# Two float32 transformer layers on one core: input sums on VectorE, T3 ahead of z, and the modulation pairs at other places

## The chip, the cores and the metric

The kernel runs on one core of a Trainium2 chip. The metric is the device time of one execution in microseconds. Before the change it is 1578.08 us, the median of three runs (1577.12 to 1578.24).

## What is computed

512 tokens of width 1024, float32, go through two layers.

```
x -> rmsnorm -> x @ w_in -> gated spatial unit, 8 heads of attention (q, k, v, gates g_a, g_b)
  -> merged @ w_out -> x + rmsnorm(.)
  -> rmsnorm -> (silu(h @ w_gate) * (h @ w_up)) @ w_down -> x + rmsnorm(.)          # first feed-forward, 2816 hidden
mod = silu(c) @ mod_w + mod_b       # 6144 values: shift1, scale1, gate1, shift2, scale2, gate2
  -> rmsnorm * (1 + scale1) + shift1 -> h @ w_in_2 -> short convolution, stick-breaking attention, SSD scan
  -> sum of three branches, each times a sigmoid gate -> @ w_o -> x + gate1 * rmsnorm(.)
  -> rmsnorm * (1 + scale2) + shift2 -> (silu(gt) * up) @ w_ffn_out -> x + gate2 * rmsnorm(.)   # second feed-forward
```

The first layer is `first_block`, the second `hybrid_layer` with its modulation vector `mod`, which depends only on `c` and so can be computed at any time before its parts are used.

## The kernel before

**Weights as a stream of units.** All large weights pass through two buffers of 8 KB per partition. A unit is loaded by SyncE into `raw`; ScalarE rounds it into `w_hi` (L1100), VectorE subtracts to get the rest, `w_lo` (L1585, semaphore `lo_done`), and TensorE multiplies in three passes, hi by hi, hi by lo and lo by hi (L2295 to L2297). A unit of 256 columns is two feature tiles of 24 matmuls each. TensorE executes its instructions in program order, and so does each other engine; semaphores tie them together. No planner is at work: the order of each engine is written out by hand.

**Feed-forward up stages.** Of the 22 units of `up` (and of `up2` in the second layer) the first four are multiplied plainly: two in `first_pair`, where token halves are interleaved with the normalisation, then two in `f_pairs`. `tile` in VectorE's `hidden` multiplies gate and up parts of one of these. The other 18 (m = 0 to 17) take seven products of 2x2 blocks instead of eight (`blocks` on TensorE, L2382 on; each product is 12 matmuls of 256 columns at L2389 to L2391). This needs sums of the input's quarters, S1 to S4 in `s_sum`, made once per stage, and sums T1 to T4 of each unit's weight blocks: T1 and T3 on VectorE (`t1_part` L1729, `t3_part` L1735), T2 and T4 on GpSimd (L993, L997). `sums_lo` (L1751) waits for both. `p1` to `p7` are the products, in the order of `pe_order`; z, c21, c22 and m are VectorE's additions of products (L1813, L1818, L1824, L1829 and L1797). Before p3 of unit m TensorE waits for c22 of m, and c22 stands behind `sums_lo` of m + 1 in VectorE's order. `dve_order` and `act_order` count these steps for the waits of other engines.

**Input sums.** Before, VectorE makes S1 (three operations, L1770 to L1772) ahead of everything else of the stage, and GpSimd makes S3, S2 and S4 (seven operations of 128x1024, L977 to L985).

**Modulation.** `mod` is computed on GpSimd in six pairs of 512 columns. `mod_begin` clears the sum and loads the bias and the first slab; each of 16 `mod_step`s loads the next slab (a GpSimd DMA, L939), waits for its own, multiplies (L957) and adds (L960). The last step of a pair raises `mod_summed`. TensorE then turns the sum (`mod_columns`, eight transposes, L2566, into banks 6 and 7) and VectorE reduces it to a column (`mod_columns`, L1700). One buffer, `mod_acc`, holds the running pair; it lies over memory that the SSD scan of the second layer uses until its last head is done. Pairs 0 and 2 give the two shift columns, pairs 1 and 3 the two scale columns; pairs 4 and 5 the gates, spread over the partitions by `mod_gate`.

**Where the pairs run before the change.** Pair 0 before the attention; pair 1 after it (eight steps, the roots of the layer norm at L1031 and L1032, five steps, then three in `blocks`); pair 2 inside the 18 units of the first up stage; pair 3 in the first down stage; pair 4 while the merge stage of the second layer runs; pair 5 inside the 18 units of the second up stage.

**Attention gates.** GpSimd adds 1 to the eight second gates (L1021) as they come, then multiplies the eight heads' outputs by them (L1024, `gated_b`). Only then does it begin pair 1.

**Merge stage.** Sixteen units: three gate units and one of the branch outputs (`branches`), four times. TensorE runs three gate units, then the first `branches`.

**Down stage and normalisation.** `post_norm` gives ScalarE's, VectorE's and GpSimd's steps around the residual additions. GpSimd's part is the roots (L894, L895). `hidden_hi` and `hidden_lo` (L1710) split hidden tiles 4 and 5 in the middle of the 18 units (at m == 8) and the others in the down stage.

## Time and profile before

| | us |
|---|---|
| median of three runs | 1578.08 |
| the profiled execution, its own time | 1577.7 |
| its span, first to last instruction | 1576.0 |
| TensorE busy | 1533.7 (97%) |
| VectorE busy | 1018.0 (65%) |
| GpSimd busy | 687.7 (44%) |
| ScalarE busy | 669.8 (43%) |
| granted TensorE clock, mean | 0.993 |

A matmul's record is longer than its distance to the next, so the busy time is no measure of speed; the waits of TensorE and the distances of its starts are. The 1.7 us between span and time lie around the program.

### The profile page before, as it was taken

How to read it: one execution, taken by the hardware profiler on the slowest of the kernel's cores; microseconds unless marked ns; L12 is line 12 of the kernel's file. 1: busy time of each engine (PE TensorE's matmuls, PEld its weight loads, DVE VectorE, ACT ScalarE, POOL GpSimd, SP SyncE). 2: the span in 40 equal slices, each digit the busy share in tenths (PEclk: the TensorE clock that was granted, in tenths of full speed). 3: DMA queues.
4: the chain of work that ended last, by engine and by line, in shares of the span. 5: the costliest groups of instructions: out<-in, count | busy, mean ns of one | idle time of the engine just before them, and what ended most of it. 6: DMA issues, size and time to landing. Idle time of an engine off the chain costs nothing.

```text
span 1576.0 us, 23248 instructions
## 1 busy us (share of the span) xinstructions
PE 1533.7 (97%) x8908; PEld 1346.1 (85%) x8908; DVE 1018.0 (65%) x1379; ACT 669.8 (43%) x1109; POOL 687.7 (44%) x543
## 2 busy tenths in 40 slices
PE   9999999979989999999999999999999899999998
PEld 9878788868889999988898888888889799999886
DVE  4342766447588999964276979643457799997423
ACT  6223444313454444442176775323236344544221
POOL 3871002760776656669120802691003666662000
PEclk9999999989999999999999999999999999999999
DMA  7532132422523434454322212443322243444231
GB/s 216 174 120 80 54 81 55 147 87 80 182 73 101 132 104 133 128 181 146 115 67 81 81 54 69 139 141 106 106 80 81 60 131 113 126 134 134 95 107 54
DMA packets 189620, 171.40 MB, mean 109 GB/s; under 512 B 20688, under 2 KB 162000, under 8 KB 189520
## 3 DMA queue, kind: packets, MB, share of 16 engines
q1 hardware_dynamic: 181456, 144.84, 30.6%
q0 software_dynamic: 8064, 25.20, 5.2%
q8 instruction: 67, 1.10, 0.3%
q14 instruction: 33, 0.27, 0.1%
HBM read 167.91 MB, written 2.10 MB: 108 GB/s over the span
## 4 chain that ended last, share of the span: by engine, by line
PE 70%; DVE 15%; POOL 9%; issue 4%; ACT 1%; DMA 0%; DVEq 0%; POOLq 0%; ACTq 0%
PE bank L2295 17%; PE bank L2297 17%; PE bank L2296 17%; POOL w_sum L997 3%; DVE w_lo L1751 3%; DVE act_m L1829 3%; POOL w_sum L993 2%; DVE w_lo L1742 2%; PE bank L2458 2%; PE bank L2459 2%; PE bank L2462 2%; DVE w_lo L1758 2%; DVE act_m L1729 1%; PE bank L2389 1%; PE bank L2616 1%
## 5 line engine op out<-in xcount | busy, mean ns | idle before, releaser
L1585 DVE TENSOR_TENSOR w_lo<-raw,w_hi 128x2048 fp32r<-128x2048 f32 (+1 forms) x109 | 216.3, 1985 | 239.4 <-ACT w_hi L1100 239.3
L2295 PE MATMUL bank<-h_hi,w_hi 128*128 128x512 f32 (+1 forms) x800 | 310.9, 389 | 11.1 <-DVE w_lo L1585 11.1
L2297 PE MATMUL bank<-h_hi,w_lo 128*128 128x512 f32 (+1 forms) x800 | 299.8, 375 | 0.0
L2296 PE MATMUL bank<-h_lo,w_hi 128*128 128x512 f32 (+1 forms) x800 | 299.6, 375 | 0.0
L1100 ACT CAST w_hi<-raw 128x2048 fp32r<-128x2048 f32 (+1 forms) x108 | 171.4, 1587 | 199.4 <-PE bank L2297 191.8
L957 POOL TENSOR_SCALAR mod_raw<-mod_raw,c_silu 128x512 f32<-128x512 f32 x96 | 197.0, 2053 | 19.3 <-DMA mod_raw<-in_mod_w 15.6
L2295 PEld LDWEIGHTS bank<-h_hi,w_hi 128*128 128x128 f32 x800 | 151.9, 190 | 40.0 <-DVE w_lo L1585 12.4
L2389 PE MATMUL bank<-s_hi,w_hi 128*128 128x256 f32 x576 | 166.7, 289 | 13.4 <-DVE act_m L1824 13.4
L2296 PEld LDWEIGHTS bank<-h_lo,w_hi 128*128 128x128 f32 x800 | 152.0, 190 | 27.4 <-issue 1.9
L2297 PEld LDWEIGHTS bank<-h_hi,w_lo 128*128 128x128 f32 x800 | 151.6, 189 | 27.7
L2391 PE MATMUL bank<-s_hi,w_lo 128*128 128x256 f32 x576 | 162.9, 283 | 0.0
L2390 PE MATMUL bank<-s_lo,w_hi 128*128 128x256 f32 x576 | 162.9, 283 | 0.0
L960 POOL TENSOR_TENSOR mod_acc<-mod_acc,mod_raw 128x512 f32<-128x512 f32 x96 | 138.1, 1438 | 8.3
L2389 PEld LDWEIGHTS bank<-s_hi,w_hi 128*128 128x128 f32 x576 | 110.2, 191 | 20.0 <-DVE act_m L1824 19.9
L2389 PE MATMUL bank<-h_hi,w_hi 128*128 128x256 f32 x432 | 122.4, 283 | 0.0
L2390 PE MATMUL bank<-h_lo,w_hi 128*128 128x256 f32 x432 | 122.2, 283 | 0.0
L2391 PE MATMUL bank<-h_hi,w_lo 128*128 128x256 f32 x432 | 122.1, 283 | 0.0
L2390 PEld LDWEIGHTS bank<-s_lo,w_hi 128*128 128x128 f32 x576 | 110.3, 192 | 0.0
L2391 PEld LDWEIGHTS bank<-s_hi,w_lo 128*128 128x128 f32 x576 | 110.3, 192 | 0.0
L2295 PE MATMUL bank<-w_hi,act_hi 128*128 128x512 f32 x280 | 109.0, 389 | 0.0
L2297 PE MATMUL bank<-w_hi,act_lo 128*128 128x512 f32 x280 | 108.9, 389 | 0.0
L2296 PE MATMUL bank<-w_lo,act_hi 128*128 128x512 f32 x280 | 108.9, 389 | 0.0
(476 smaller groups left out, 3348.3 us busy)
## 6 DMA issues: line engine op xcount, KB each, us to landing
raw<-in_w_in SPq DMA_DIRECT2D x102, 512.0 KB, 4.5
mod_raw<-in_mod_w POOLq DMA_DIRECT2D x96, 256.0 KB, 3.0
raw<-in_w_ffn_in SPq DMA_DIRECT2D x44, 512.0 KB, 4.9
raw<-in_w_gate SPq DMA_DIRECT2D x22, 512.0 KB, 4.0
raw<-in_w_up SPq DMA_DIRECT2D x22, 512.0 KB, 5.3
raw<-in_w_down SPq DMA_DIRECT2D x20, 512.0 KB, 4.5
raw<-in_w_ffn_out SPq DMA_DIRECT2D x20, 512.0 KB, 4.5
raw<-in_w_out SPq DMA_DIRECT2D x8, 512.0 KB, 4.3
```

Of the source, the lines that this page charges most:

```text
L957: then(gp.tensor_scalar(mod_raw[:, s, :], mod_raw[:, s, :], c_silu[:, k:k + 1], None, ALU.mult))
L960: ins = gp.tensor_tensor(acc, acc, mod_raw[:, s, :], ALU.add)
L997: gp.tensor_tensor(t4, t2, quarter_of(n, 1, 0), ALU.subtract).then_inc(block_pool, 1)
L1100: ins = act.copy(w_hi[s][:, cols], raw[s][:, cols])
L1585: ins = dve.tensor_tensor(w_lo[s][:, cols], raw[s][:, cols], w_hi[s][:, cols].bitcast(F32), ALU.subtract)
L1751: dve.tensor_tensor(operand_pair(w_lo, n0, 2), operand_pair(w_sum, n0, 2), operand_pair(w_hi, n0, 2).bitcast(F32), ALU.subtract).then_inc( ...
L2295: pe.matmul(o, st_hi, mv_hi, start=first, stop=False)
L2296: pe.matmul(o, st_hi, mv_lo, start=False, stop=False)
L2297: return pe.matmul(o, st_lo, mv_hi, start=False, stop=last)
L2389: pe.matmul(o, hi[:, k, :], mv_hi(k), start=first and k == 0, stop=False, skip_group_check=not first)
L2390: pe.matmul(o, hi[:, k, :], mv_lo(k), start=False, stop=False, skip_group_check=not first)
L2391: ins = pe.matmul(o, lo[:, k, :], mv_hi(k), start=False, stop=k == 3, skip_group_check=not first)
```

## The change

The input sums S1, S2 and S4 are made by VectorE, S1 behind the lo part of the stage's third unit, S2 and S4 behind that of the fourth; GpSimd keeps S3, and the last of its three operations waits for the third unit's lo part. In the loop of the 18 units VectorE makes T3 ahead of z. Hidden tiles 4 and 5 are split at the start of the down stage. GpSimd applies each gate as soon as its head is there. The modulation pairs move: nine steps of pair 1 ahead of the layer norm's roots, four behind, three in units m = 1 to 3 of the first loop; pair 2 in the first down stage; pair 3 between the SSD scan and pair 4, with two steps ahead of the scan's root and fourteen behind it; pair 5 begins behind the second layer's gate with four steps ahead of `post_norm(2)`, and its other twelve stand in m = 1 to 12 of the second loop. TensorE's and VectorE's `mod_columns` move accordingly: pair 1 at the end of the first loop, pair 2 in the first down stage, pair 3 directly ahead of the first `branches`.

```diff
-            yield from ("s1", "s1_lo", "s3_lo", "s24_lo", "t1 0", "t3 0", "pair 0", "sums 0", "t4 0", "t1_lo 0")
+            yield from ("s1", "s3_lo", "t1 0", "s24", "t3 0", "s1_lo", "pair 0", "s24_lo", "sums 0", "t4 0", "t1_lo 0")
...
-                yield from [f"t1 {ahead}"] if ahead else []
+                yield from [f"t1 {ahead}", f"t3 {ahead}"] if ahead else []
                 yield f"z {m}"
-                yield from [f"t3 {ahead}"] if ahead else []
...
-            def blocks(n0, which, c):
+            def blocks(n0, which, c, pair, done):
...
+                gp.wait_ge(lo_done, n0 + 3)
                 gp.tensor_tensor(s3, s3, h_quarter(h_lo, 1, 0), ALU.subtract).then_inc(block_pool, 1)
-                wait_dve(gp, which, "s1")
-                gp.tensor_tensor(s2, s1, h_quarter(h_hi, 0, 0), ALU.subtract).then_inc(block_pool, 1)
-                wait_pool_sum(gp, which, 2)
-                then(gp.tensor_tensor(s2, s2, h_quarter(h_lo, 0, 0), ALU.subtract))
-                then(gp.tensor_tensor(s4, h_quarter(h_hi, 0, 1), s2, ALU.subtract))
-                gp.tensor_tensor(s4, s4, h_quarter(h_lo, 0, 1), ALU.add).then_inc(block_pool, 1)
...
+                    if 1 <= m <= 2 * KD - done:
+                        mod_step(pair, done + m - 1)
...
                 then(gp.tensor_scalar(gates[:, KD + f, :], gates[:, KD + f, :], 1.0, None, ALU.add))
-            for f in range(KD):
                 gp.wait_ge(head_out, f + 1)
                 gp.tensor_tensor(q_t[:, f, :], q_t[:, f, :], gates[:, KD + f, :], ALU.mult).then_inc(gated_b, 1)
             mod_begin(1)
-            for i in range(8):
+            for i in range(9):
                 mod_step(1, i)
...
-            blocks(n_up, 0, 1)
-            mod_pair(3)
+            blocks(n_up, 0, 1, 1, 13)
+            mod_pair(2)
             post_norm(1)
...
+            mod_begin(3)
+            for i in range(2):
+                mod_step(3, i)
             gp.wait_ge(ms2_ready, 1)
...
+            for i in range(2, 2 * KD):
+                mod_step(3, i)
             mod_pair(4)
             mod_lo_part(4)
+            mod_begin(5)
+            for i in range(4):
+                mod_step(5, i)
             post_norm(2)
-            blocks(n_up2, 1, 3)
+            blocks(n_up2, 1, 3, 5, 4)
...
-                    if units == 6 and 1 <= j <= 4:
-                        for t in range(4 * j + 2, 4 * j + 6):
+                    if units == 6 and j <= 4:
+                        for t in range(4 if j == 0 else 4 * j + 2, 4 * j + 6):
...
-                    if m == 2 and which == 0:
-                        dve.wait_ge(small_in, 16 * (SMALL + SMALL_2))
-                        mod_columns(1, gain_3, True)
-                    if m == 8:
-                        hidden_lo(which, PLAIN)
-                        hidden_lo(which, PLAIN + 1)
...
             split(n_mg + 4)
+            mod_columns(3, gain_4, True)
             merge(n_mg, 0, 0, STILL)
...
             pe.wait_ge(ssm_lo_done, 4)
-            pe.wait_ge(mod_out, 4)
-            branches(n_mg + 3, STILL)
+            mod_columns(3)
+            branches(n_mg + 3, STILL, 4)
```

## Rows read from the trace of the kernel before

**Rows 1.** Page, part 1: busy time, share of the span and instructions of each engine.
```profile
PE 1533.7 (97%) x8908; PEld 1346.1 (85%) x8908; DVE 1018.0 (65%) x1379; ACT 669.8 (43%) x1109; POOL 687.7 (44%) x543
```

**Rows 2.** Waits of TensorE: line and releaser, us in total, times, longest.
```profile
PE bank L2389 <- DVE act_m L1824: 13.4, 32, 1.3
PE bank L2295 <- DVE w_lo L1585: 11.1, 2, 6.6
PE bank L2660 <- DVE v_sgu L1945: 9.0, 1, 9.0
```

**Rows 3.** Timeline of GpSimd, 820 to 1200 us: start, duration, instruction, idle before.
```profile
979.37 3.21 POOL L1069 TENSOR_TENSOR z_t<-z_t 128x512 f32<-128x512 f32 x1
...
990.92 1.68 POOL L1071 TENSOR_TENSOR rr_ssm<-ms_ssm,power 128x8 f32<-128x8 f32 x1 [8.34 <-DVE ms_ssm L2238]
992.55 0.96 POOL L944 MEMSET mod_acc<- 128x1024 f32 x1
...
1000.31 1.57 POOL L957 TENSOR_SCALAR mod_raw<-mod_raw,c_silu 128x512 f32<-128x512 f32 x1 [4.30 <-DMA mod_raw<-in_mod_w]
...
1004.19 2.65 POOL L957 TENSOR_SCALAR mod_raw<-mod_raw,c_silu 128x512 f32<-128x512 f32 x1
...
1069.12 1.70 POOL L960 TENSOR_TENSOR mod_acc<-mod_acc,mod_raw 128x512 f32<-128x512 f32 x1
```

**Rows 4.** Timeline of TensorE, 985 to 1020 us: first matmul of the first branch unit.
```profile
1012.94 0.39 PE L2295 MATMUL bank<-sb_hi,w_hi 128*128 128x512 f32 x1
```

**Rows 5.** Windows: stretch, length, busy of PE, PEld, DVE, ACT, POOL, PEclk, DMA, GB/s.
```profile
461.00:470.00 9.00, 8.49 (x30) 6.85 (x31) 8.34 (x5) 1.25 (x2) 8.84 (x3) 0.81 0.44 118
```

**Rows 6.** Timeline of GpSimd, 215 to 360 us: gate products and pair 1.
```profile
284.35 14.14 POOL L1024 TENSOR_TENSOR q_t<-q_t,gate_a 128x512 f32<-128x512 f32 x8
...
337.79 1.26 POOL L960 TENSOR_TENSOR mod_acc<-mod_acc,mod_raw 128x512 f32<-128x512 f32 x1
```

**Rows 7.** Timeline of VectorE, 280 to 362 us: the last head's output.
```profile
286.14 0.69 DVE L1898 COPY q_t<-bank 128x512 f32<-128x512 f32 x1 [3.30 <-PE bank L2639]
```

**Rows 8.** Timeline of TensorE: first matmul of the third unit, both up stages.
```profile
461.51 0.67 PE L2295 MATMUL bank<-h_hi,w_hi 128*128 128x512 f32 x1 [4.42 <-DVE w_lo L1585]
...
1232.15 0.80 PE L2295 MATMUL bank<-h_hi,w_hi 128*128 128x512 f32 x1 [6.63 <-DVE w_lo L1585]
```

**Rows 9.** Timeline of VectorE, 440 to 540 us: an operation of S1.
```profile
448.08 3.31 DVE L1771 TENSOR_TENSOR s_sum<-s_sum,h_lo 128x1024 f32<-128x1024 f32 x1
```

**Rows 10.** Timeline of VectorE and GpSimd inside the first loop.
```profile
498.25 0.42 DVE L1829 TENSOR_TENSOR act_m<-act_m,silu_t 128x256 f32<-128x256 f32 x1
...
536.03 1.72 DVE L1735 TENSOR_TENSOR w_sum<-raw 128x512 f32<-128x512 f32 x1
...
539.01 1.23 DVE L1751 TENSOR_TENSOR w_lo<-w_sum,w_hi 128x1024 fp32r<-128x1024 f32 x1 [0.93 <-POOL w_sum L997]
...
541.75 1.34 POOL L960 TENSOR_TENSOR mod_acc<-mod_acc,mod_raw 128x512 f32<-128x512 f32 x1
541.86 1.51 DVE L1829 TENSOR_TENSOR act_m<-act_m,silu_t 128x256 f32<-128x256 f32 x1
```

**Rows 11.** Timeline of TensorE, 535 to 560 us: the end of p2 and the start of p3.
```profile
539.95 0.28 PE L2390 MATMUL bank<-h_lo,w_hi 128*128 128x256 f32 x1
540.07 0.28 PE L2391 MATMUL bank<-h_hi,w_lo 128*128 128x256 f32 x1
540.62 0.39 PE L2389 MATMUL bank<-s_hi,w_hi 128*128 128x256 f32 x1 [0.28 <-DVE act_m L1824]
```

**Rows 12.** Chain of waits in order of time: T2 of two neighbouring units around m = 8.
```profile
578.32 1.31 POOL w_sum L993
...
590.12 1.30 POOL w_sum L993
```

**Rows 13.** Timelines around the second layer's output projection: gate product, first root.
```profile
1165.94 0.39 PE L2574 MATMUL bank<-mod_lo,ones_r 128*128 128x512 f32 x1
...
1186.19 0.32 POOL L894 TENSOR_SCALAR sq_y<-sq_y 128x1 f32<-128x1 f32 x1 [23.77 <-ACT y_out L1106]
```

More of the change, by code:

```diff
@@ L672, in act_order @@
         def act_order():
-            yield from ("s1_hi", "s3_hi", "s24_hi", "pair 0", "sums 0", "p1 0", "t4 0", "t1 0")
+            yield from ("s3_hi", "s1_hi", "pair 0", "s24_hi", "sums 0", "p1 0", "t4 0", "t1 0")
             for m in range(BLOCKS):
@@ L694, in wait_pool @@
         def wait_pool(eng, which, m, total):
-            eng.wait_ge(block_pool, (2 * BLOCKS + 3) * which + 2 * m + 3 + total)
-        def wait_pool_sum(eng, which, done):
-            eng.wait_ge(block_pool, (2 * BLOCKS + 3) * which + done)
+            eng.wait_ge(block_pool, (2 * BLOCKS + 1) * which + 2 * m + 1 + total)
         POST_UNIT = [n_out + 3, n_dn + 11, n_out2 + 3, n_dn2 + 11]
@@ L1033, in _ @@
             gp.wait_ge(merged, KD)
-            for i in range(8, 13):
+            for i in range(9, 13):
                 mod_step(1, i)
             post_norm(0)
-            blocks(n_up, 0, 1)
-            mod_pair(3)
+            blocks(n_up, 0, 1, 1, 13)
+            mod_pair(2)
             post_norm(1)
@@ L1251, in hidden @@
                 split(n0 + 2)
-                wait_dve(act, which, "s1")
-                act.copy(s_hi[:, S1], s_sum[:, S1]).then_inc(block_act, 1)
-                wait_pool_sum(act, which, 1)
+                wait_pool(act, which, 0, 0)
                 act.copy(s_hi[:, S3], s_sum[:, S3]).then_inc(block_act, 1)
@@ L1257, in hidden @@
                 split(n0 + 3)
-                wait_pool_sum(act, which, 3)
-                act.copy(s_hi[:, S2:S4 + 1], s_sum[:, S2:S4 + 1]).then_inc(block_act, 1)
+                wait_dve(act, which, "s1")
+                act.copy(s_hi[:, S1], s_sum[:, S1]).then_inc(block_act, 1)
                 tile(n0 + 2, act_hi[:, 2, :], 0, STILL)
                 pair_hi(0)
+                wait_dve(act, which, "s24")
+                act.copy(s_hi[:, S2:S4 + 1], s_sum[:, S2:S4 + 1]).then_inc(block_act, 1)
                 sums_hi(0)
@@ L1638, in post_norm @@
                 for j in range(units):
-                    if units == 6 and 1 <= j <= 4:
-                        for t in range(4 * j + 2, 4 * j + 6):
+                    if units == 6 and j <= 4:
+                        for t in range(4 if j == 0 else 4 * j + 2, 4 * j + 6):
                             hidden_lo(k // 2, t)
@@ L1772, in hidden @@
                 dve.tensor_tensor(s1, s1, h_quarter(h_lo, 1, 1), ALU.add).then_inc(block_dve, 1)
-                tile(n0, 0, 0)
-                split(n0 + 2)
-                wait_act(dve, which, "s1_hi")
-                wait_pool_sum(dve, which, 2)
-                dve.tensor_tensor(s_lo[:, S1], s1, s_hi[:, S1].bitcast(F32), ALU.subtract).then_inc(block_dve, 1)
+                tile(n0 + 1, 1, 1)
                 wait_act(dve, which, "s3_hi")
                 dve.tensor_tensor(s_lo[:, S3], s_sum[:, S3], s_hi[:, S3].bitcast(F32), ALU.subtract).then_inc(block_dve, 1)
-                tile(n0 + 1, 1, 1)
                 split(n0 + 3)
+                t1_part(0)
+                wait_dve(dve, which, "s1")
+                then(dve.tensor_tensor(s2, s1, h_quarter(h_hi, 0, 0), ALU.subtract))
+                then(dve.tensor_tensor(s2, s2, h_quarter(h_lo, 0, 0), ALU.subtract))
+                then(dve.tensor_tensor(s4, h_quarter(h_hi, 0, 1), s2, ALU.subtract))
+                dve.tensor_tensor(s4, s4, h_quarter(h_lo, 0, 1), ALU.add).then_inc(block_dve, 1)
+                tile(n0 + 2, 2, 0)
+                t3_part(0)
+                wait_act(dve, which, "s1_hi")
+                dve.tensor_tensor(s_lo[:, S1], s1, s_hi[:, S1].bitcast(F32), ALU.subtract).then_inc(block_dve, 1)
+                pair_lo(0)
                 wait_act(dve, which, "s24_hi")
@@ L2437, in blocks @@
                     product(m, 6, "x", *sums(S4), first=False)
-                    if m == 0 and which == 0:
-                        mod_columns(1)
             def token_unit(n, x_hi, x_lo, k0, first, last, pace, width=512, tiles=range(NT)):
@@ L2561, in mod_columns @@
                 pe.wait_ge(mod_summed, pair + 1)
-                if pair == 2:
-                    pe.wait_ge(mod_out, 2)
                 for q in range(KD):
@@ L2848, in gate_unit, with branches @@
                     feature_tile(n, f, pace)
-            def branches(n, pace):
+            def branches(n, pace, columns=0):
                 u = UNITS[n]
@@ L2857, in branches @@
                     wait(pe, emptied[2 + f], u["round"] + pace.by(pace.rounds))
+                    if f == 1:
+                        wait(pe, mod_out, columns)
                     for b, k0, x_hi, x_lo, kt in ((4 + 2 * f, 2, sb_hi, sb_lo, 2), (5 + 2 * f, 4, ssm_hi, ssm_lo, 4), (2 + f, 0, sc_hi, sc_lo, 2)):
```

41 lines of the change are left out of this document (11 added, 30 removed).

## The prediction

> **What bounds the kernel now.** I read the page first, then who waited for whom, then the timelines at each wait, and last the chain. TensorE is busy for 97% of the span [rows 1], so what can be won is the time it stands, and what can be lost is a new stand. Its waits are few [rows 2]: 32 short ones before p3 (13.4 us, 0.42 us each), one at the third unit of either up stage (11.1 us), and one before the spatial products (9.0 us). The timelines say what makes each, and the code says which new waits stand in TensorE's own order. There is one, and it decides.
>
> **1. Pair 3 ahead of the first branch unit (the largest term, a loss).** TensorE now turns pair 3 directly ahead of the first `branches`, and that wait wants all 16 steps of it. GpSimd can't begin before its last square sum of the SSD scan, which ends at 979.37 + 3.21 = 982.6 us [rows 3]: `mod_acc` lies over the scan's states, and it is one in-order queue. TensorE reaches the first branch unit at 1012.9 us [rows 4], only 30 us later. What GpSimd has to do in between:
> - Begin: from clearing the sum to the first product 1000.31 - 992.55 = 7.8 us, of which 4.3 are the wait for the slab [rows 3]. Bounds 3.5 and 7.8; I take 7.8, the same act ten microseconds later.
> - The root for the scan, now in the midst of it: 1.7 us [rows 3].
> - Sixteen steps. Pair 4 took from 1000.31 to 1069.12 + 1.70, 70.5 us, 4.4 a step; the first was 3.9 from the next [rows 3]. The longer ones have VectorE's lo parts beside them. For most of this stretch TensorE and so VectorE will stand, so I take 3.9 and add three collisions of about 1 us, without the last step's load: 64.8 us. Bounds 62 and 70.5.
> Together 982.6 + 7.8 + 64.8 + 1.7 = 1056.9 us in the old frame, bounds 1049.8 and 1062.6. TensorE waits 1056.9 - 1012.9 = 44.0 us (37 to 50). The eight transposes are only moved. Behind TensorE's wait are queued the whole merge stage and all that follows; nothing covers it. The root's delay of some 6 us, which VectorE and TensorE wait for, ends inside this stand and costs nothing more.
> After a stand the granted clock is at its lower level of 1.2 GHz for a while: 0.81 in mean over the 9 us behind the wait of 4.4 us [rows 5], so 9 x 0.19 = 1.7 us are lost. I add 1.7. Sum of the part: **+45.7 us**.
>
> **2. The gates head by head.** Before, the eight products start behind the last gate and end at 284.35 + 14.14 = 298.5 us, 1.8 each [rows 6]. Seven of them can now be done earlier; the last waits for the last head, 286.14 + 0.69 = 286.8 us [rows 7], and ends at 288.6. Pair 1 begins 9.9 us earlier, but one more step (4.1) is in front of the roots, so GpSimd turns to them 5.8 us earlier than 337.79 + 1.26 = 339.1 us [rows 6]. TensorE's wait of 9.0 us [rows 2] falls to 3.2. Then TensorE is late by that still, as GpSimd's roots are last again. **-5.8 us**, bounds 3.5 (more collisions, as the steps meet other VectorE work) and 10.7 (the wait and the slow clock behind it gone).
>
> **3. The input sums.** VectorE's S1 operations, 3.31 us beside GpSimd's [rows 9], leave the way of the third unit. Its lo part can then be ready when TensorE is done with the pair, where the two waits began, at 461.51 - 4.42 = 457.1 and 1232.15 - 6.63 = 1225.5 us [rows 8]. That would save their 11.1 us [rows 2] and the slow clock behind each, 1.7 as above [rows 5]: 14.5 us. But the work is not gone. Between that point and the first p3, VectorE now has seven operations of 1024 columns at 1.2 us (the lo part of the sums, [rows 10]) = 8.6, where it had three, and its two-input operations collide: one with S3's last operation, which now waits for the same lo part (2.1 us, 3.31 - 1.2), two with T2 and T4 (1 us each, as T3's 1.72 in [rows 10] against 0.7 for its size). With the tiles, lo parts and first operands that were always there I get an estimated 30 us of VectorE work until p7 of the first unit. TensorE has 96 matmuls of 512 columns at 0.23 us (twice the 0.12 of 256 columns, [rows 11]) and 24 of 256 to do until then, 25 us. VectorE is late by about 5 us, shared out over p1, p7, p6, p5 and p3, of which about 0.3 a stage were there before: 14.5 - 10.0 + 0.6 is **-5.1 us** (bounds 0 and 14.5). The new wait on GpSimd queues S3's last operation and T2 of unit 0 behind it; ScalarE waits for S3 ahead of the second tile, which is in the 5 us.
>
> **4. The loops.** One unit is 84 matmuls, 0.12 us apart [rows 11] = 10.08 us. TensorE loses 540.62 - 540.07 - 0.12 = 0.43 us before p3 and another 0.1 on the restart, 0.53 in all, so a unit takes 10.61. The reason is a ring: T4 on GpSimd, the lo part of the sums (it stood 0.93 us for T4), c22, and back over a step of a pair: VectorE's L1829 takes 1.51 us because GpSimd's add holds it up, and 0.42 where no step runs [rows 10]. Without a step T1, T2 and T4 come 1.1 us earlier, more than the 0.53 that are missing, and TensorE is the bound. Steps stood in 16 units of either loop; now in 3 and in 12. In the first loop 13 stands go, in the second 4: 17 x 0.53 = 9.0 us. The next ring, over the weights' load and the first operands' lo part, I take to be shorter than 10.08 us; rival two says what it costs if it isn't.
> The two hidden tiles at m == 8 made that unit 590.12 - 578.32 = 11.80 us long [rows 12], 1.2 above its neighbours, in both loops: -2.4. The column of pair 1 at m == 2 is two operations of the same 512 columns, so 1.2 again: -1.2. All of these return in the down stage, where TensorE's plain units keep it busy for 10.9 us each and VectorE has only their lo part to make; they cost nothing there, and without that cover the same 3.6. Since small waits for loads will take back a part I count 12.2 of the 12.6. Sum **-12.2 us**, bounds 5 and 13.
>
> **5. T3 ahead of z.** T3 took 1.72 us since it met T2 on GpSimd [rows 10]. Put first it takes about 0.7, but T2 then starts behind it. T4 ends when T1, T3, T2 and T4 are through one after the other, whichever goes first: 0, bounds -0.2 and +0.2 a unit in the 15 units with a step, 3 us in all. z moves back by 0.6 us and TensorE's p5 waits for it; no wait of TensorE at z is in the trace [rows 2]. By the Trainium skill (SBUF — State Buffer, on the shared port pair) a VectorE operation with two SBUF inputs and a GpSimd operation exclude each other for a whole instruction. That gives the 0 above; were it a sharing of bandwidth, T3 alone first would give each unit up to 1 us, 3 + 12 units at most 0.53 = 8 us. The durations here, 0.42 or 1.51 for one operation, speak for the lock.
>
> **6. Pair 5's four steps ahead of post_norm(2).** They can begin when the gate product is read, 1165.94 + 0.39 = 1166.3 us, and take 7.8 + 4 x 4 = 23.8 us, to 1190.1; the first root was asked for at 1186.19 [rows 13]. Four microseconds late, of which part is slack: **+0.5 us**, bounds 0 and 3.
>
> **The sum.** 45.7 + 0.5 - 5.8 - 5.1 - 12.2 = +23.1 us on the profiled execution's 1577.7 us: 1600.8. It stood 0.4 below the median of the runs, 1578.08, so 1601.2; I say **1601 us**.
>
> **Rivals.**
> - **TensorE does not stand for pair 3, the other side.** If GpSimd had pair 3 summed when TensorE arrives, the gains alone would be left: 1577.7 - 23.1 + 0.5 = 1555.1 us. The place is the wait ahead of the first branch unit, the price 45.7 us. It decides from the point at which 16 steps fit in 30 us, that is 1.4 us a step with a begin of 7.8; the shortest distance of two steps is 3.9 [rows 3]. For it speaks only that I could have misread what the wait counts. Chance 0.04.
> - **The stand comes, the gains don't.** VectorE, with the sums back, keeps the start of both loops late by all that it saved, and the loops stay at 10.6 us by another ring (the raw load's), so that only the gates' 5.8 and the 3.6 are won: 1577.7 + 46.2 - 9.4 = 1614.5 us. Chance 0.12. For it: VectorE stood only 0.93 us a unit [rows 10], so it has little to spare. Against it: where L1829 took 0.42 us TensorE did not stand in that unit, and only 32 of 36 units have the wait [rows 2].
> - **The stand is shorter and the gains full.** 38.7 us by the low bounds, gains 30: 1586 us. Chance 0.06.
>
> **How the numbers follow.** The forecast case has 0.78. Its own bounds (37 to 50 us of stand, gains of 17 to 30) reach from about 1588 to 1612; both extremes at once are unlikely. The range 1589 to 1615 takes in the second rival and leaves out the first, most of the third and the tails. Below 0.2% (3.2 us, about what a measurement of this kernel can tell from no change) lie only the first rival and a part of what I have not thought of: faster 0.05, same 0.01, slower 0.94.
>
> **What would show it.** In the changed kernel's profile: a wait of TensorE of 37 to 50 us at the transposes L2566's line, released by GpSimd's L960, and a granted clock of 0.5 behind it; the wait before the spatial products at 3 us; none at the third units, but some at the first products of the loops; units of 10.08 us from m = 4 on in the first loop and from 13 on in the second, 10.6 before. The forecast is wrong if TensorE's largest wait isn't the one at pair 3, or if it is far from 44 us.

## The result, and the profile after

The changed kernel takes **1604.74 us** (median of four runs, 1604.25 to 1605.91) beside 1577.63 us for the kernel before on the same chip. The ratio is 1.0173, with an interval of 1.0155 to 1.019: 27.1 us slower, where 1601 us had been forecast. The profiled execution spans 1602.5 us, at a mean granted TensorE clock of 0.984.

Page of the changed kernel, part 1 (busy time, share of the span and instructions of each engine), which answers to [rows 1]:

```profile
PE 1531.8 (96%) x8908; PEld 1344.2 (84%) x8908; DVE 963.6 (60%) x1387; ACT 672.4 (42%) x1109; POOL 654.4 (41%) x535
```

VectorE and GpSimd are less busy than before, by 54 and 33 us. Eight operations have moved from GpSimd to VectorE, which is quicker at them (in the first stage the four took 2.4 to 4.3 us on GpSimd before and take 1.2 to 2.2 on VectorE now), and fewer of the two engines' operations meet. The time is longer all the same. Who waited for whom, TensorE alone, in the changed kernel (line and releaser, us in total, times, longest), to be read beside [rows 2]:

```profile
PE bank L2542 <- POOL mod_acc L954: 37.6, 1, 37.6
PE bank L2369 <- DVE act_m L1808: 6.9, 16, 0.8
PE bank L2636 <- DVE v_sgu L1923: 6.6, 1, 6.6
PE bank L2855 <- DVE rr_diag L2221: 3.1, 1, 3.1
PE bank L2369 <- DVE w_lo L1723: 2.4, 2, 1.2
PE bank L2369 <- ACT act_m L1258: 2.2, 2, 1.1
PE bank L2559 <- POOL ident L882: 1.6, 1, 1.6
PE bank L2369 <- ACT silu_t L1231: 1.3, 2, 0.7
...
PE bank L2369 <- DVE w_lo L1732: 0.5, 2, 0.2
```

The first line is the new stand: TensorE's transposes of pair 3 wait for GpSimd's last add. Of the old waits the two at the third units (11.1 us) are gone, the 32 before p3 have become 16, and the one before the spatial products fell from 9.0 to 6.6. New are 3.1 us before the products that spread the SSD root, and the four last kinds at L2369, all at the first products of either loop.

TensorE runs the same 8908 instructions in both kernels and only `mod_columns` moves. So the account can be made from the start of one and the same matmul in either trace, and the difference. Timeline of TensorE in the changed kernel (start, duration, instruction, idle before):

```profile
343.94 3.76 PE L2636 MATMUL bank<-w_sp_t,v_sgu 128*128 128x128 f32 x16 [6.59 <-DVE v_sgu L1923]
...
487.62 0.39 PE L2369 MATMUL bank<-h_hi,w_hi 128*128 128x256 f32 x1 [1.08 <-ACT act_m L1258]
...
991.29 2.56 PE L2855 MATMUL bank<-rr_diag,ones 128*128 128x128 f32 x16 [3.10 <-DVE rr_diag L2221]
...
1043.46 1.94 PE L2542 MATMUL bank<-ident,mod_acc 128*128 128x128 f32 x8 [37.62 <-POOL mod_acc L954]
1045.05 0.78 PE L2275 MATMUL bank<-sb_hi,w_hi 128*128 128x512 f32 x1
```

| matmul | before | after | after less before | term of the sum | forecast | found |
|---|---|---|---|---|---|---|
| output of attention, nothing changed yet | 261.9 | 262.9 | +1.0 | (scatter) | 0 | +1.0 |
| spatial products | 345.0 | 343.9 | -1.1 | gates | -5.8 | -2.1 |
| third unit, ten matmuls in | 465.3 | 457.9 | -7.4 | | | |
| first loop, behind its starting waits | 490.8 | 487.6 | -3.2 | sums, stage one | | -2.1 |
| last p3 of the first loop | 669.5 | 657.4 | -12.2 | first loop | | -9.0 |
| first branch unit, six matmuls in | 1014.1 | 1047.3 | +33.2 | pair 3 | +45.7 | +45.4 |
| third unit of the second stage, ten in | 1235.7 | 1260.7 | +24.9 | | | |
| second loop, behind its starting waits | 1261.8 | 1290.6 | +28.8 | sums, stage two | (both) -5.1 | -4.4 |
| last p3 of the second loop | 1428.9 | 1455.5 | +26.6 | second loop | (both) -12.2 | -2.2 |

Between pair 3 and the second stage's third unit the difference stays at +33.2: pair 5's four steps cost nothing (0.5 forecast). The found terms add up to 26.6 us; the two spans differ by 26.5. Eight transposes (0.8 us at full clock) have left the first loop, and eight now stand ahead of the first branch unit. So 0.8 of the loop's 9.0 us and 0.8 of pair 3's 45.4 are work that moved, neither won nor lost.

### The profile page after: what moved, and what is told of

It reads as the page before. It is cut to its first block and busy times, and to the rows that moved or that the text cites. A ratio compares the mean times of both kernels' runs of the same rounds, so it can differ in the third digit from the quotient of the medians.

```text
span 1602.5 us, 23250 instructions
## 1 busy us (share of the span) xinstructions
PE 1531.8 (96%) x8908; PEld 1344.2 (84%) x8908; DVE 963.6 (60%) x1387; ACT 672.4 (42%) x1109; POOL 654.4 (41%) x535
## 5 line engine op out<-in xcount | busy, mean ns | idle before, releaser
L1566 DVE TENSOR_TENSOR w_lo<-raw,w_hi 128x2048 fp32r<-128x2048 f32 (+1 forms) x109 | 212.7, 1952 | 232.4 <-ACT w_hi L1084 232.3
L951 POOL TENSOR_SCALAR mod_raw<-mod_raw,c_silu 128x512 f32<-128x512 f32 x96 | 193.2, 2012 | 21.7 <-DMA mod_raw<-in_mod_w 17.9
L2369 PE MATMUL bank<-s_hi,w_hi 128*128 128x256 f32 x576 | 165.4, 287 | 8.7 <-DVE act_m L1808 6.9
L980 POOL TENSOR_TENSOR w_sum<-raw,act_m 128x512 f32<-128x512 f32 x36 | 55.1, 1529 | 227.7 <-PE bank L2371 150.2
L2369 PE MATMUL bank<-h_hi,w_hi 128*128 128x256 f32 x432 | 122.6, 284 | 4.5 <-DVE w_lo L1723 2.4
L2369 PEld LDWEIGHTS bank<-s_hi,w_hi 128*128 128x128 f32 x576 | 110.3, 192 | 12.8 <-DVE act_m L1808 10.1
```

Of the source, the lines that this page charges most:

```text
L951: then(gp.tensor_scalar(mod_raw[:, s, :], mod_raw[:, s, :], c_silu[:, k:k + 1], None, ALU.mult))
L980: gp.tensor_tensor(t2, quarter_of(n, 1, 1), four(t1_sum(m)), ALU.subtract).then_inc(block_pool, 1)
L1566: ins = dve.tensor_tensor(w_lo[s][:, cols], raw[s][:, cols], w_hi[s][:, cols].bitcast(F32), ALU.subtract)
L2369: pe.matmul(o, hi[:, k, :], mv_hi(k), start=first and k == 0, stop=False, skip_group_check=not first)
```

## The experiments

Each kernel was timed beside the kernel before on its own chip, where that took 1579 to 1580 us instead of 1577.6; so ratios are given, and for parts of a few microseconds the starts of the same matmuls in two traces, as above.

**1. The root's delay inside the stand** (run root_first), from the changed kernel:

```diff
             mod_begin(3)
-            for i in range(2):
-                mod_step(3, i)
             gp.wait_ge(ms2_ready, 1)
             gp.tensor_tensor(rr_ssm[:], ...).then_inc(rr_ready, 1)
...
-            for i in range(2, 2 * KD):
+            for i in range(2 * KD):
                 mod_step(3, i)
```

> The changed kernel with the root of the SSD norm ahead of all sixteen steps of pair 3 instead of behind two of them; GpSimd does the same work in another order. In the changed kernel's trace TensorE waits 3.1 us for that root and runs about 1.6 us slower behind the wait, and then stands 37.6 us for pair 3. Theory A, as in the prediction (the root's delay ends inside the stand): the end of the stand is set by GpSimd's queue alone, so TensorE arrives 4.7 us earlier and stands 4 to 5 us longer (41 to 43 us); the time stays at 1604.7 us within 1. Rival B (the two waits are paid one after the other): 4.7 us less, 1600.0 us.

Measured: 1604.74 us (1603.67 to 1606.76), ratio 1.0165 [1.0147, 1.0183]. TensorE's waits in it:

```profile
PE bank L2540 <- POOL mod_acc L954: 43.7, 1, 43.7
```

The wait for the root is gone and the stand has grown from 37.6 to 43.7 us, by 6.1. Of these, 5.0 are what the root cost (3.1 us of wait and 1.9 by which the matmuls behind it fell back further, a short lag and then the lower clock), 0.8 come from a TensorE that was already ahead when it reached the root, and 0.3 from a pair that ended later. Behind the stand the starts of the same matmuls agree to 0.1 us in the two traces. So a wait ahead of a stand is free, as the prediction said, and theory B falls. It also says that the stand can't be shortened from TensorE's side: its end is GpSimd's.

**2. The transposes 33 us later** (run cols_later). The first turn of the merge's loop is written out on TensorE and VectorE, and pair 3's column stands in it:

```diff
-            mod_columns(3)
-            branches(n_mg + 3, STILL, 4)
-            with pe.Fori(0, 3) as p:
+            branches(n_mg + 3, STILL)
+            for g in range(3):
+                gate_unit(n_mg + 4 + g, STILL)
+            mod_columns(3)
+            branches(n_mg + 7, STILL, 4)
+            with pe.Fori(0, 2) as p:
```

> The changed kernel with TensorE's transposes of pair 3 and VectorE's column of it moved behind the next three gate units of the merge (33 us later); GpSimd's order stays. Theory A (the stand is the whole of the loss, and the gains stand by themselves): 40.7 us go (37.6 of wait and 3.1 of slow clock behind it), 1604.7 - 40.7 = 1564.0 us, range 1562 to 1568. Pair 4 then ends about 1127 us, ahead of its gate product near 1158. Rival B (the stand had covered GpSimd's and VectorE's work, which now meets in the merge stage; a wait comes back at the new place or at pair 4's gate product): 1575 us or more, with a wait of 10 us or more there.

Measured: 1565.78 us (1563.66 to 1566.63), ratio 0.9911 [0.9894, 0.9929]; from the changed kernel's 1.0173 that is 41 us, and by the starts of the same matmuls 39.4. TensorE's longest waits:

```profile
PE bank L2373 <- DVE act_m L1808: 7.5, 16, 1.1
PE bank L2640 <- DVE v_sgu L1923: 6.6, 1, 6.6
PE bank L2859 <- DVE rr_diag L2221: 3.1, 1, 3.1
```

The transposes in its timeline:

```profile
1050.21 1.09 PE L2546 MATMUL bank<-ident,mod_acc 128*128 128x128 f32 x8
```

The transposes come at 1050.21, GpSimd's last add ended at 1050.16, and TensorE's unit before them at 1050.15. So there is no stand, but only just: here the pair ends 7 us later than in the changed kernel, and 33 us of delay were barely enough. There is none at pair 4's gate product either. One wait was the whole loss, and the gains stand by themselves: the changed kernel with this one edit is faster than the kernel before.

**3. Both edits** (run cols_later_root_first), the two diffs together.

> Both edits: pair 3's transposes behind three gate units, and the root ahead of all steps. Theory A: without the stand the root's 3.1 us of wait and 1.6 us of slow clock are on TensorE's path and now go: 4.7 us less than with the transposes alone, 1559.3 us. Sixteen steps end near 1043 us and TensorE comes at about 1047, so no new wait. Rival B (what the root costs is paid by the later steps, pair 3 ends behind TensorE's arrival): no less than with the transposes alone, 1564 us or more, with a wait at the transposes.

Measured: 1566.83 us (1565.83 to 1568.65), ratio 0.9923 [0.9905, 0.994]. Theory B:

```profile
PE bank L2544 <- POOL mod_acc L954: 5.8, 1, 5.8
```

The root's 3.1 us are gone and 5.8 us at the transposes have come. I had counted pair 3's steps as in the stand, with VectorE mostly silent. Here VectorE works on in the merge stage, the steps collide with it, and the pair ends at 1048.5 us instead of 1043. Run root_first has the same operations in the same order: from clearing the sum to the last add they took 74.1 us there, where VectorE was silent from 1010 to 1040 us, and 79.9 us here. The length of a GpSimd chain depends on what VectorE does beside it.

**4. All pairs where they were, the other edits kept** (run pairs_back):

```diff
-                    if 1 <= m <= 2 * KD - done:
-                        mod_step(pair, done + m - 1)
+                    if which == 0:
+                        if m == 0:
+                            mod_step(1, 14)
+                            mod_step(1, 15)
+                        elif m == 1:
+                            mod_begin(2)
+                        else:
+                            mod_step(2, m - 2)
+                    elif m == 0:
+                        mod_begin(5)
+                    elif m <= 2 * KD:
+                        mod_step(5, m - 1)
```

> The changed kernel with every modulation pair where it was before (pair 1's last steps, pair 2 and pair 5 in the loops, pair 3 in the down stage, eight steps ahead of the attention's roots, pair 1's column at the third unit), but with the other edits kept: gates head by head, input sums, T3 ahead of z, the two hidden tiles out of the ninth unit. Theory A (the parts add up): gates about 6.6 less since only eight steps stand ahead of the roots, sums 6.5, hidden tiles 2.4, T3 0: 1577.6 - 15.5 = 1562 us, range 1559 to 1566, with units of 10.6 us wherever a step runs. Rival B (T3 ahead of z is what shortens the units, not the steps' absence): units of 10.1 to 10.3 us with steps in them and 1550 to 1556 us. Rival C (the gains at the start of the loops need GpSimd free of steps there): 1567 us or more.

Measured: 1565.3 us (1563.43 to 1568.44), ratio 0.9913 [0.9891, 0.9934], 14.3 us less than the kernel before; 15.5 had been expected. TensorE's waits:

```profile
PE bank L2374 <- DVE act_m L1812: 12.7, 32, 0.8
PE bank L2374 <- DVE w_lo L1727: 3.8, 2, 2.6
PE bank L2645 <- DVE v_sgu L1930: 2.7, 1, 2.7
```

The p3 of three neighbouring units of the first loop, in TensorE's timeline:

```profile
555.77 0.39 PE L2374 MATMUL bank<-s_hi,w_hi 128*128 128x256 f32 x1 [0.33 <-DVE act_m L1812]
566.44 0.39 PE L2374 MATMUL bank<-s_hi,w_hi 128*128 128x256 f32 x1 [0.34 <-DVE act_m L1812]
577.11 0.39 PE L2374 MATMUL bank<-s_hi,w_hi 128*128 128x256 f32 x1 [0.34 <-DVE act_m L1812]
```

With the steps back the 32 waits are back, and a unit takes 10.67 us although T3 stands ahead of z. That refutes theory B and shows what shortened the units: the missing steps. Against the kernel before, the first loop gains 0.2 us here, 9.0 in the changed kernel. The start of stage one, counted from where the clock is full again behind the spatial products, keeps only 0.1 us of the sums' gain, against 1.9 with the steps gone (one first product waits 2.64 us for its lo part): a part of theory C.

**5. Seven steps ahead of the attention's roots** (run seven_steps), on top of run cols_later:

```diff
-            for i in range(9):
+            for i in range(7):
                 mod_step(1, i)
...
-            for i in range(9, 13):
+            for i in range(7, 11):
                 mod_step(1, i)
...
-            blocks(n_up, 0, 1, 1, 13)
+            blocks(n_up, 0, 1, 1, 11)
```

> On top of the kernel with pair 3's transposes moved later (run cols_later): seven steps of pair 1 ahead of the attention's roots instead of nine, four behind the merge of the first output, five instead of three in the first loop. It tests what term 2 of the prediction missed: the gates' edit gave 2.4 us of wait where 5.8 were forecast, because the ninth step took 5.9 us and not 4.1. Theory A (GpSimd's roots alone set that wait): TensorE's wait of 6.6 us before the spatial products goes to below 0.5, the slow clock behind it too, about 7.0 less there; two more steps in the loop cost at most 2 x 0.53 = 1.1 us. 5.9 us less than cols_later in all, 1560 us beside a kernel before at 1579.6. Rival B (VectorE's or ScalarE's chain is right behind the roots): the wait stays above 2.5 us, and the gain is below 3.5 us.

Measured: 1557.7 us (1557.38 to 1558.72), ratio 0.9869 [0.9852, 0.9885]. By the traces the spatial products start 6.5 us earlier, 1.9 more come back with the clock behind them, and the loop's two steps cost 0.9: 7.5 us at the end of the first loop. Further on the trace gains another 1.6 us that this edit doesn't explain. It has the same wait of 3.1 us for the SSD root, but the granted clock does not fall behind it (the mean there is 1.00; the same stretch of the changed kernel, 985 to 995 us, has 0.88). Windows as in [rows 5]:

```profile
978.00:988.00 10.00, 6.91 (x39) 5.72 (x38) 7.40 (x12) 3.00 (x3) 9.45 (x7) 1.00 0.48 148
```

That makes 9.1 us by the traces, 6.6 by the ratios. Theory A: GpSimd's roots alone set the wait, and nothing else is close behind them.

**6. One step ahead of the SSD root, the transposes in the midst of the branch unit** (run one_step_split), on top of run cols_later:

```diff
-            for i in range(2):
-                mod_step(3, i)
+            mod_step(3, 0)
...
                     if f == 1 and columns:
+                        mod_columns(3)
                         wait(pe, mod_out, columns)
```

> On top of cols_later: one step of pair 3 ahead of the SSD root instead of two, and TensorE's transposes between the two halves of the next branch unit instead of ahead of it (5.5 us later). With no step ahead of the root and the transposes where they were, the wait for the root went and one of 5.8 us at the transposes came. Theory A: the root is given at about 982 us instead of 986.4, so the 3.1 us of wait and 1.6 us of slow clock go; pair 3 ends near 1050 as before, TensorE comes to the transposes at 1051; in their place it waits some 2 us for VectorE's sum of the columns, which banks 6 and 7 need. 2.5 to 3 us less than cols_later. Rival B (the wait for VectorE's columns or pair 3's end takes it all back): no difference.

Measured: 1560.95 us (1560.36 to 1561.87), ratio 0.989 [0.9873, 0.9906]. Timeline of TensorE:

```profile
1047.56 1.03 PE L2545 MATMUL bank<-ident,mod_acc 128*128 128x128 f32 x8
1050.18 0.50 PE L2278 MATMUL bank<-sb_hi,w_hi 128*128 128x512 f32 x1 [1.58 <-DVE gain L1684]
```

The wait for the root is gone, that for VectorE's column is 1.58 us. Behind the attention stage the traces differ by 3.0 us (a shorter wait before the spatial products comes on top, in which the two kernels are the same); the ratios differ by 0.0021, 3.3 us: theory A.

**7. T3 behind z again** (run t3_back on top of run cols_later, and run best_t3_back on top of run best, below):

```diff
                         t1_part(m + 1)
-                        t3_part(m + 1)
...
                     dve.tensor_tensor(g[:, 256:512], region(m, "x"), mid[:, 256:512], ALU.add).then_inc(block_dve, 1)
+                    if m + 1 < BLOCKS:
+                        t3_part(m + 1)
```

> cols_later with T3 of the next unit behind z again, as in the kernel before; all else kept. Theory A (as in the prediction, T3's place is worth nothing): the same time within 1 us, units without a step stay at 10.08 us. Rival B (the units' 0.53 us came from T3 being ahead, not from the missing steps): units of 10.6 us again, 9 us or more slower than cols_later.

Measured: 1561.84 us (1560.92 to 1563.26), ratio 0.9895 [0.9878, 0.9911]. The units without a step keep their 10.08 us, so T3's place is not what shortened them; but this is less than cols_later, not more (2.5 us by the ratios), and by its trace 1.4 of it lie in the loops (0.5 in the first, 1.0 in the second). The more exact pair of runs:

> The kernel of run best with T3 behind z again. The earlier run t3_back came out 3.9 us below cols_later, but its trace gives T3 behind z at most 1.0 us, all in the second loop, and the rest lies in the attention stage, where the kernels are the same. Theory A (T3's place is worth 1 us at most): 0 to 1.2 us less than best. Rival B (T3 ahead of z costs what the earlier medians differ by): 3 to 4 us less.

Measured: 1553.34 us (1552.6 to 1553.46), ratio 0.9835 [0.9822, 0.9849], beside 1555.28 for run best: 1.9 us. By the traces 0.4 us come in the first loop and 1.0 in the second. One unit of the second loop in run best, VectorE and GpSimd:

```profile
1275.69 0.68 DVE L1715 TENSOR_TENSOR w_sum<-raw 128x512 f32<-128x512 f32 x1
...
1279.08 1.22 DVE L1731 TENSOR_TENSOR w_lo<-w_sum,w_hi 128x1024 fp32r<-128x1024 f32 x1 [1.91 <-POOL w_sum L984]
...
1275.90 1.63 POOL L980 TENSOR_TENSOR w_sum<-raw,act_m 128x512 f32<-128x512 f32 x1 [3.42 <-DVE act_m L1709]
1277.67 1.30 POOL L984 TENSOR_TENSOR w_sum<-w_sum,raw 128x512 f32<-128x512 f32 x1
```

And the same unit in run best_t3_back:

```profile
1273.34 1.72 DVE L1716 TENSOR_TENSOR w_sum<-raw 128x512 f32<-128x512 f32 x1
...
1276.31 1.22 DVE L1732 TENSOR_TENSOR w_lo<-w_sum,w_hi 128x1024 fp32r<-128x1024 f32 x1 [0.92 <-POOL w_sum L985]
...
1273.22 1.29 POOL L981 TENSOR_TENSOR w_sum<-raw,act_m 128x512 f32<-128x512 f32 x1 [3.42 <-DVE act_m L1710]
1274.65 1.56 POOL L985 TENSOR_TENSOR w_sum<-w_sum,raw 128x512 f32<-128x512 f32 x1
```

T3 ahead saves VectorE a microsecond (0.68 us instead of 1.72), but T2 then takes 1.63 us instead of 1.29. T2 and T4 together need 3.07 us against 2.99, and VectorE only waits longer for T4, 1.91 us instead of 0.92. A unit with a step takes 10.67 us with T3 ahead and 10.60 with T3 behind.

**8. The input sums as before** (run sums_back), on top of run cols_later: S2 and S4 on GpSimd, S1 ahead of the third unit's lo part.

```diff
-                gp.wait_ge(lo_done, n0 + 3)
                 gp.tensor_tensor(s3, s3, h_quarter(h_lo, 1, 0), ALU.subtract).then_inc(block_pool, 1)
+                wait_dve(gp, which, "s1")
+                gp.tensor_tensor(s2, s1, h_quarter(h_hi, 0, 0), ALU.subtract).then_inc(block_pool, 1)
+                wait_pool_sum(gp, which, 2)
+                then(gp.tensor_tensor(s2, s2, h_quarter(h_lo, 0, 0), ALU.subtract))
+                then(gp.tensor_tensor(s4, h_quarter(h_hi, 0, 1), s2, ALU.subtract))
+                gp.tensor_tensor(s4, s4, h_quarter(h_lo, 0, 1), ALU.add).then_inc(block_pool, 1)
```

> cols_later with the input sums as in the kernel before (S2 and S4 on GpSimd, S1 ahead of the third unit's lo part on VectorE); all else kept. From the two traces the input sums' edit was worth 2.1 us in the first and 4.4 us in the second up stage. Theory A: 6.5 us more than cols_later, with waits of 4.4 and 6.6 us at the third units and none worth naming before the first p1. Rival B (with no steps in the loop's head, the old order would have cost less in the first stage): 4 to 5 us more. Rival C (VectorE pays back all of it): no difference.

Measured: 1569.33 us (1568.25 to 1571.68), ratio 0.9942 [0.9924, 0.996]; the ratios differ by 0.0031, 4.9 us. TensorE's waits:

```profile
PE bank L2286 <- DVE w_lo L1577: 11.0, 2, 6.6
```

The third units wait again, and the starting waits of the loops are gone, as theory A had it. By the starts of the same matmuls the edit is worth 1.9 us up to the first loop and 4.5 up to the second. But with the sums on VectorE the first units of the loops are longer, by 0.3 and 0.7 us, so that 1.6 and 3.8 are left, 5.4 in all. The size lies between A (6.5) and B (4 to 5), and the ratios' 4.9 us is B's.

**9. The sum of it** (run best): the edits of runs cols_later, one_step_split and seven_steps together.

> All that the runs so far speak for: the changed kernel with pair 3's transposes between the halves of the second branch unit, one step ahead of the SSD root, and seven, four and five steps of pair 1. Theory A (the parts add up, each sits at its own wait): seven_steps' 1557.7 us less the 3.4 us that the traces give one_step_split behind the attention: 1554.3 us beside a kernel before at 1578.9, a ratio of 0.984 to 0.986. Rival B (a later wait takes part of it back, since GpSimd has pair 4's 16 steps and the gate product still ahead): 1556 us or more.

Measured: **1555.28 us** (1555.2 to 1556.04), ratio 0.9848 [0.9835, 0.9861]. The parts add up to a microsecond. What is missing is no later wait, as rival B has it: in the trace of run seven_steps the slow clock behind the root was already absent, so that one_step_split's edit could win only 1.2 us there by the traces, not 3.0. With T3 behind z the kernel takes 1553.34 us, 26 us less than the kernel before.

**10. The gates behind the last head again** (run best_gates_back):

```diff
                 then(gp.tensor_scalar(gates[:, KD + f, :], gates[:, KD + f, :], 1.0, None, ALU.add))
+            for f in range(KD):
                 gp.wait_ge(head_out, f + 1)
```

> The kernel of run best with the eight gate products behind the last gate again. Theory A (GpSimd's queue sets the roots, and the products come 6.5 us later there: they end at 298.4 us in the kernel before and at 291.9 with the edit): with seven steps pair 1's part ends near 335.2 us where the first root is wanted at 332.0, so a wait of some 3.1 us comes back before the spatial products, and about 1 us of slow clock: 4 us more than best (3.5 to 5). Rival B (the full 6.5 us and slow clock): 7 us more or above. Rival C (the gates' edit is worth nothing, the step count is all): no difference.

Measured: 1561.47 us (1561.07 to 1562.89), ratio 0.9889 [0.9873, 0.9904], 6.2 us more than run best. TensorE's longest wait:

```profile
PE bank L2640 <- DVE v_sgu L1923: 4.7, 1, 4.7
```

The gate products on GpSimd:

```profile
284.54 14.15 POOL L1001 TENSOR_TENSOR q_t<-q_t,gate_a 128x512 f32<-128x512 f32 x8
```

The mechanism is theory A's (a wait at the spatial products, set by GpSimd), the size nearer to B's: 4.7 us of wait and 2.1 of lag and slow clock behind it. The first root begins at 335.28 us, as A had said, but this execution came to the attention stage 1.0 us ahead of run best, and so waited that much longer. With the gates' edit and seven steps the wait is 0.1.

**11. The two hidden tiles back in the ninth unit** (run best_hidden_back):

```diff
+                    if m == 8:
+                        hidden_lo(which, PLAIN)
+                        hidden_lo(which, PLAIN + 1)
```

> The kernel of run best with the two hidden tiles made in the ninth unit of either loop again, as in the kernel before. From the traces the edit gave 1.2 us at that unit of the first loop beyond what the missing step gave, and 0.8 us at the second. Theory A: 2.0 us more (1.5 to 2.5). Rival B (in the first loop no step runs in that unit, so it has 0.6 us to spare): 0.6 + 0.8 = 1.4 us more. Rival C (the tiles, now back out of the down stage, free TensorE there from a wait): no difference or less than best.

Measured: 1556.78 us (1556.32 to 1558.27), ratio 0.9856 [0.9841, 0.9871], 1.5 us more. TensorE in the second loop:

```profile
1343.07 0.39 PE L2378 MATMUL bank<-s_hi,w_hi 128*128 128x256 f32 x1 [0.44 <-DVE silu_t L1801]
1346.98 0.39 PE L2378 MATMUL bank<-s_hi,w_hi 128*128 128x256 f32 x1 [0.77 <-DVE act_m L1810]
```

The second comes 11.86 us behind the p3 of the unit before, where run best has 10.65: the tiles cost 1.2 us. In the first loop nothing moves at all: where no step runs, VectorE has room for the two tiles. The total is B's, by another split.

## Why the prediction held, step by step

**Pair 3** was forecast at +45.7 us and found at 45.4. GpSimd's timeline in the changed kernel gives each piece:

```profile
970.29 0.96 POOL L938 MEMSET mod_acc<- 128x1024 f32 x1
...
977.04 2.17 POOL L951 TENSOR_SCALAR mod_raw<-mod_raw,c_silu 128x512 f32<-128x512 f32 x1 [3.29 <-DMA mod_raw<-in_mod_w]
...
985.62 1.68 POOL L1050 TENSOR_TENSOR rr_ssm<-ms_ssm,power 128x8 f32<-128x8 f32 x1
...
1002.83 1.29 POOL L954 TENSOR_TENSOR mod_acc<-mod_acc,mod_raw 128x512 f32<-128x512 f32 x1
...
1006.71 1.27 POOL L954 TENSOR_TENSOR mod_acc<-mod_acc,mod_raw 128x512 f32<-128x512 f32 x1
...
1042.05 1.26 POOL L954 TENSOR_TENSOR mod_acc<-mod_acc,mod_raw 128x512 f32<-128x512 f32 x1
```

Begin 977.04 - 970.29 = 6.8 us (7.8 forecast from [rows 3]), root 1.7, and the rest of the way to 1043.3, 64.6 us, for the steps (64.8 forecast). The chain was 1.3 us shorter than forecast. Where VectorE is silent two steps are 3.9 us apart, as in the one place of [rows 3] from which I took it. So the chain of an in-order engine could be laid out from another pair's rows, moved to its new place. Against the stand of 44.0 us the page of waits shows 37.6 at the transposes and 3.1 at the root, 40.7 together; run root_first shows that these are one sum. The root's wait had lag and slow clock of its own behind it, 1.9 us, ahead of the stand: 42.6 us, 1.4 below the forecast, which is the shorter chain. TensorE just behind the stand, windows (length, busy of PE, PEld, DVE, ACT, POOL, granted clock, DMA share, GB/s), to compare with [rows 5]:

```profile
1044.00:1047.00 3.00, 3.00 (x12) 2.61 (x11) 1.45 (x3) 0.00 (x0) 1.19 (x2) 0.50 0.01 3
```

It ran at 0.50, the lower level of 1.2 GHz, after the stand of 37.6 us. Beyond the stand itself the difference of the starts grew by 2.9 us. The eight transposes are 0.8 of these, work that came from the first loop (they took 1.6 us here, 1043.46 to 1045.05, and 0.8 at full clock), so the slow clock cost 2.1, not 1.7. Like for like pair 3 cost 44.6 us. That 45.4 stands so near to 45.7 is in part luck: the chain was 1.3 us shorter, the clock 0.4 dearer, and 0.8 are the transposes, which the sum had as only moved.

**The gates** were the term that was mis-sized: -5.8 forecast, -2.1 found, outside its own bounds of 3.5 to 10.7. GpSimd in the changed kernel:

```profile
288.31 3.20 POOL L1000 TENSOR_TENSOR q_t<-q_t,gate_a 128x512 f32<-128x512 f32 x1 [2.80 <-DVE q_t L1876]
291.46 0.95 POOL L938 MEMSET mod_acc<- 128x1024 f32 x1
...
338.08 0.23 POOL L1007 TENSOR_SCALAR mean_var<-mean_var 128x1 f32<-128x1 f32 x1
```

The last product had been priced at the mean of eight, 1.8 us. It took 3.20, since it meets VectorE; seven others took 1.3. It ends at 291.5, not 288.6; 1.0 of these 2.9 us is the scatter of the first line of the table. Then nine steps took 46.6 us, where eight before took 40.7 [rows 6] and one more had been priced at 4.1: 1.8 us more than forecast. 1.9 and 1.8 us are the 3.7 that were missing. It isn't the ninth step that was dear. In run pairs_back eight steps stand at the new, earlier place, and they take 42.8 us there, 2.1 more than the same eight before; nine take 46.6 us in two profiled executions and 45.0 in five others. So what was wrong is the price of a step: it had been carried over from the old place, and VectorE's work beside the new place is other. That the roots were the bound, and GpSimd's queue what set them, was right (runs seven_steps and best_gates_back).

**The input sums** were forecast at -5.1 us, found at -6.5 in the changed kernel's trace up to the loops; run sums_back finds 5.4, with what the first units behind give back. The waits of the third units went, and VectorE was late by 4.2 and 3.9 us at the first products, not 5 a stage.

**The loops** were forecast at -12.2 us and found at -11.2, or -10.4 without the transposes that left the first loop. The first gave 8.2 so counted, where 13 x 0.53, the column and the tiles had been put at 9.3. One reading was wrong here: in the kernel before, TensorE waited before p3 in 15 units of the first loop, not in 16, for its units m = 1 and 2 took 10.08 us, and with 3 such waits in the changed kernel 12 went and not 13. T3 has most of the rest, see below. TensorE's p3 of five units of the second loop in the changed kernel:

```profile
1415.00 0.39 PE L2369 MATMUL bank<-s_hi,w_hi 128*128 128x256 f32 x1 [0.74 <-DVE act_m L1808]
...
1425.18 0.38 PE L2369 MATMUL bank<-s_hi,w_hi 128*128 128x256 f32 x1
1435.35 0.28 PE L2369 MATMUL bank<-s_hi,w_hi 128*128 128x256 f32 x1
1445.43 0.28 PE L2369 MATMUL bank<-s_hi,w_hi 128*128 128x256 f32 x1
1455.51 0.28 PE L2369 MATMUL bank<-s_hi,w_hi 128*128 128x256 f32 x1
```

These are 10.18, 10.17, 10.08 and 10.08 us apart, close to the 10.08 that were forecast for units without a step. The second loop gave 2.2 where 3.3 were counted, and **T3**, counted at nothing, is what took the rest: run best_t3_back finds 1.0 us there and 0.4 in the first loop. The bound for it had been 0.2 us a unit either way; it is 0.07. The ring over GpSimd was read rightly, and the attribution of the hidden tiles only in part: they cost 1.2 us where a step runs beside them, and nothing in the first loop once the steps are gone, so the two gains of that unit are not added but shared.

In favour of the exclusive port that the prediction drew from the Trainium skill (SBUF — State Buffer, Who interferes with whom) speak the rows of experiment 7: T3 took 0.68 us and T2 0.34 longer than its 1.29, or T2 took 1.29 and T3 1.04 longer than its 0.68. Whoever starts first keeps its own duration, and the other waits for it.

**Pair 5** cost 0, inside its bounds of 0 to 3. Of the rivals, the first (no stand) is what run cols_later is: 1555.1 us was worked out for it, and it took 1565.8, or some 1564 on the first chip's scale. The profiled execution of it lies 11 us above that sum. By its starts 5.0 of them are the root's wait and the slow clock behind it, which count once there is no stand to hide them; 3.3 are the gates', 2.3 the loops', 1.8 scatter from ahead of the spatial products, and 0.4 a lag at the transposes' new place, less 1.4 that the sums gave more and 0.5 that pair 5 did not cost. The medians are 9 us apart. The other rivals did not come. (The low end of the forecast's own bounds is 1586 us by its terms, as in the third rival, not 1588.)

The whole was forecast at +23.1 us and the traces show +26.6. The gates' 3.7, the loops' 1.0 and 1.0 of scatter went one way, the sums' 1.4, pair 5's 0.5 and pair 3's 0.3 the other; that the total missed by only 3.5 us owes something to this.

## What to carry to other kernels

A new wait of the bounding engine is worth looking at before anything else: find what its releaser must still do, in its own order, from the last act that frees its memory, and lay the times end to end; here one wait in the wrong place turned a gain of 14 us (run cols_later) into a loss of 27. The cure was not less work but a later consumer: the column isn't needed until `post_norm(2)`, and any place behind GpSimd's end is free. Where that end lies has to be worked out for the new place: without the stand VectorE works on, and the same chain ended 7 us later. And a delay ahead of a stand is free only while the stand is there; take the stand away, and such delays (here 5.0 us) come to light.

## What was not expected of the hardware

- An operation of GpSimd beside VectorE's is not a fixed number: the last gate product took 3.20 us and the seven before it 1.3, the same step of a pair 3.9 or 5 to 6 us. The mean of a group, here 1.8 us for the gate products, is no price for the one that counts.
- What a wait cost beyond its own length, in lag and slow clock, did not grow with it. At the spatial products it was 1.4 us behind a wait of 2.7 us (run pairs_back), 1.5 and 2.6 behind waits of 4.9 (one_step_split and cols_later_root_first), 1.8 behind 6.6 (cols_later) and 1.8 behind 9.0 (the kernel before). At the third units it was 1.7 behind 4.4 and 2.1 behind 6.6 (sums_back), at the transposes 2.1 behind 37.6.
- The granted clock does not fall behind every such wait. Behind the same 3.1 us for the SSD root the wait cost 1.9 us more in the traces of the changed kernel, cols_later and sums_back, and 0.3 in those of seven_steps and t3_back, where the clock stayed at 1.00. What decides it stays open.
- With the same code up to there, the wait at the spatial products with nine steps ahead of the roots was 6.6 us in two profiled executions, 4.9 in four and 4.7 in one. GpSimd's nine steps took 46.6 us in the first two and 45.0 in the other five. So its chain fell into one of two patterns of collisions, 1.7 us apart, and what decides which one stays open.
